# Where in an expert's pass the next expert's tokens are gathered and its registers loaded

## What is computed

```python
D_MODEL, SEQ, N_EXPERTS, TOP_K, D_FF_2 = 1024, 256, 32, 4, 1024
logits = t @ w_router + b_router
top_val, top_idx = lax.top_k(logits, TOP_K)
gate_w = jax.nn.softmax(top_val, axis=-1)
# for every expert e, over the tokens that chose it:
hb = xb @ w_exp_in[e] + b_exp_in[e]             # 1024 -> 2048
g = jnp.minimum(hb[:, :D_FF_2], 7.0)
u = jnp.clip(hb[:, D_FF_2:], -7.0, 7.0)
a = g * jax.nn.sigmoid(1.702 * g) * (u + 1.0)
y_e = a @ w_exp_out[e] + b_exp_out[e]           # 1024 -> 1024
# y[token] = sum over its 4 experts of gate_w * y_e
```

## Time and profile before

| | |
|---|---|
| time, median of 3 runs | 1464.12 us (1462.02 to 1468.61) |
| time of the profiled execution | 1462.36 us |
| span of the profiled execution | 1460.5 us |
| granted TensorE clock, mean over the span | 0.974 |
| PE busy | 1306.9 us, 89% of the span |
| DVE, ACT, POOL busy | 466.8, 504.1, 221.5 us |
| transfers | 494.40 MB, mean 339 GB/s |

### The profile page before, as it was taken

How to read it: one execution, slowest core, us unless ns; L and a number is a source line. 1 busy time by engine, 2 the same in 40 slices (tenths; PEclk the granted TensorE clock), 3 DMA queues, 4 the chain that set the end, 5 groups by cost and what they waited for, 6 DMA issues and landing times.

```text
span 1460.5 us, 25988 instructions
## 1 busy us (share of the span) xinstructions
PE 1306.9 (89%) x9475; PEld 810.3 (55%) x9476; DVE 466.8 (32%) x916; ACT 504.1 (35%) x790; POOL 221.5 (15%) x129
## 2 busy tenths in 40 slices
PE   7999999999999997787889898989888988898886
PEld 7787999878999853333333433344343434343433
DVE  2755777664534961111101110111011111111112
ACT  5566666555657422112111311131121212131222
POOL 6772122007774300000000000000000000000000
PEclk9999999999999999999999989999999999999999
DMA  9432667755463778999999999999999999999996
GB/s 342 171 101 64 185 186 234 281 194 182 165 231 116 270 331 373 431 432 430 431 431 404 431 431 431 415 432 431 431 431 431 420 431 431 431 418 431 431 431 268
DMA packets 105321, 494.40 MB, mean 339 GB/s; under 512 B 6609, under 2 KB 56129, under 8 KB 80481
## 3 DMA queue, kind: packets, MB, share of 16 engines
q1 hardware_dynamic: 103795, 491.50, 82.8%
q10 hardware_dynamic: 1486, 2.34, 0.4%
HBM read 492.76 MB, written 1.06 MB: 338 GB/s over the span
## 4 chain that ended last, share of the span: by engine, by line
PE 61%; DMA 25%; DVE 5%; ACT 4%; issue 3%; POOL 1%; SPq 0%; DVEq 0%; ACTq 0%; POOLq 0%
DMA big_mem<-in_w_exp_in 25%; PE ps L1071 18%; PE ps L1115 8%; PE ps L595 6%; PE ps L597 5%; PE ps L596 5%; PE ps L1054 3%; PE ps L1129 1%; PE ps L813 1%; PE ps L814 1%; PE ps L815 1%; PE ps L1138 1%; PE ps L1102 1%; ACT x L1740 1%; PE ps L615 1%
## 5 line engine op out<-in xcount | busy, mean ns | idle before, releaser
L1071 PE MATMUL ps<-big_mem,ring_mem 128*32 128x512 f32 (+1 forms) x2304 | 375.7, 623 | 46.5 <-DMA big_mem<-in_w_exp_in 46.4
L1071 PEld LDWEIGHTS ps<-big_mem,ring_mem 128*32 128x32 f32 (+1 forms) x2304 | 115.1, 124 | 288.6 <-issue 212.5
L1115 PE MATMUL ps<-big_mem,x 128*32 128x256 f32 (+1 forms) x1888 | 183.4, 436 | 4.7 <-ACT x L1740 3.7
L595 PE MATMUL ps<-hT_hi,w_hi 128*128 128x256 f32 x600 | 171.3, 285 | 1.3 <-DVE hT_lo L1836 1.3
L1724 ACT ACTIVATE ring_mem<-ring_mem 128x256 f32<-128x256 f32 (+1 forms) x36 | 17.7, 493 | 441.6 <-DVE ring_mem L2344 441.6
L596 PE MATMUL ps<-hT_lo,w_hi 128*128 128x256 f32 x600 | 169.7, 283 | 0.0
L597 PE MATMUL ps<-hT_hi,w_lo 128*128 128x256 f32 x600 | 169.7, 283 | 0.0
L1054 PEld LDWEIGHTS ps<-ring_mem,h 128*128 128x128 f32 x1024 | 124.0, 191 | 57.8 <-issue 57.8
L2344 DVE TENSOR_SCALAR ring_mem<-ps 128x256 f32<-128x256 f32 (+1 forms) x36 | 18.7, 520 | 406.6 <-PE ps L1071 406.6
L1795 ACT ACTIVATE big_mem<-ahead 128x2048 f32<-128x2048 f32 x62 | 115.0, 1902 | 85.2 <-DMA ahead<-in_w_exp_in 82.6
L1054 PE MATMUL ps<-ring_mem,h 128*128 128x96 f32 x1024 | 141.6, 281 | 0.0
(11 more groups left out here) (431 smaller groups left out, 1748.9 us busy)
## 6 DMA issues: line engine op xcount, KB each, us to landing
big_mem<-in_w_exp_in SPq DMA_DIRECT2D x97, 2048.0 KB, 23.1
big_mem<-in_w_exp_out SPq DMA_DIRECT2D x64, 2048.0 KB, 19.0
ahead<-in_w_exp_in SPq DMA_DIRECT2D x31, 2048.0 KB, 21.7
ring_mem<-in_w_in SPq DMA_DIRECT2D x14, 2048.0 KB, 7.7
ring_mem<-in_w_up SPq DMA_DIRECT2D x44, 512.0 KB, 4.9
ring_mem<-in_w_down SPq DMA_DIRECT2D x5, 2048.0 KB, 10.7
ring_mem<-in_w_out SPq DMA_DIRECT2D x4, 2048.0 KB, 7.7
ring_mem<-in_w_branch_a SPq DMA_DIRECT2D x1, 2048.0 KB, 7.3
```

The costliest lines, as they stand in the source:

```text
L595: mm(out, hi, x_hi, start=start, stop=False)
L1071: last = mm(out, stationary, weights[:, f, w * q:w * (q + 1)] if m > XS else weights[:, :, w * q:w * (q + 1)], start=start, stop=stop)
L1115: last = mm(ps[m * q:m * (q + 1), 4 + at // XS, 0:w], aT[:, k % n, k // n, :], wout[:, k, w * q:w * (q + 1)], start=(k == 0), stop=(k == K ...
```

## The change

Of `gather(0, EARLY)`, blocks 0 to 2 stay where they were; block 3 goes between `way_back` and `turn_a`, block 4 behind `turn_a`. Block 5 moves from ahead of `second` to behind it, blocks 6 and 7 both behind `combine`. `load_next` goes from behind the first gather to the very end of the pass. ACT copies blocks 0 to 4 after `a_in` rather than after the first sigmoid. No work is added or taken away.

```diff
@@ PE, one_pass
                 pe.wait_ge(s["picks_ready"], turn + 2)
-                gather(0, EARLY)
-                load_next()
+                gather(0, 3)
                 for b, (at, m) in enumerate(blocks):
                     pe.wait_ge(s["source_ready"], base + b + 1)
                     pe.wait_ge(s["u_ready"], base + b + 1)
                     way_back(b, at)
+                gather(3, EARLY - 1)
                 for b, (at, m) in enumerate(blocks):
                     pe.wait_ge(s["back_ready"], base + b + 1)
                     pe.wait_ge(s["a_ready"], base + b + 1)
                     turn_a(at, m)
+                gather(EARLY - 1, EARLY)
+                pe.wait_ge(s["aT_ready"], base + len(blocks))
+                second(blocks, landed_all)
                 pe.wait_ge(s["xT_ready"], 2 * turn + 3)
                 gather(EARLY, EARLY + 1)
-                pe.wait_ge(s["aT_ready"], base + len(blocks))
-                second(blocks, landed_all)
-                gather(EARLY + 1, EARLY + 2)
                 for b, (at, m) in enumerate(blocks):
                     pe.wait_ge(s["y_ready"], base + b + 1)
                     combine(b, at, m, base + b)
-                gather(EARLY + 2, KD)
+                gather(EARLY + 1, KD)
+                load_next()
                 pe.reg_add(base_reg, base_reg, len(blocks))
@@ ACT, one_pass
                 sigmoid(base, *blocks[0])
-                tokens_in(0, EARLY, 2 * turn + 3)
                 for b, (at, m) in enumerate(blocks):
...
                 for b, (at, m) in enumerate(blocks):
                     a_in(base + b, at, m)
+                tokens_in(0, EARLY, 2 * turn + 3)
```

## The result

| | before | after |
|---|---|---|
| time, median of 7 runs each, measured together | 1466.08 us | 1469.06 us (1468.34 to 1474.04) |
| ratio, after to before | | 1.0037, 95% interval 1.0021 to 1.0053 |
| profiled execution: time, span | 1462.36, 1460.5 us | 1471.93, 1470.1 us |
| granted TensorE clock, mean over the span | 0.974 | 0.949 |

The change makes the kernel slower by 0.37%, between 0.2 and 0.5%, some 3 to 8 us; I had forecast 1475 in a range of 1457 to 1489.

The account below looks back on a forecast made before the run. Weights bound the expert stage (907 us), PE having some 85 us to spare; after the change PE's 859 + 64 for the clock, 938 with stops and bias, give 1473.3 profiled, 1475 us predicted, range 1457 to 1489.

Parts of the forecast that it names:

- The gain between the matmuls: Between a pass's two matmuls, fewer gather rows and no load issue: -1.7, -1.15, -0.75 us for 32, 64, 96 slots.
- The loss at the end: At the pass's end, uncovered register loads delay the next pass: +2.7, +2.1, +3.0 us for 32, 64, 96 slots.
- Rival 2: At pass boundaries the loads stay covered: boundary grows at most 0.7 us, holes close, 1458 us; chance 0.08.
- PE becomes the bound: Expert stage: PE's 859 us plus 64 for the clock give 923 us, against 907 for the weights.
- nearly level: Expert stage: PE and weights nearly level, each sometimes waiting for the other; +11 us on the profiled execution.
- Rival 3: PE falls clearly behind the weights, every pass losing 3.0 us to the clock at its start: 1505 us; chance 0.06.
- rival 1: Expert stage: weights stay the bound if the clock mostly holds, holes shrink: -3.6 us, 1459 us; chance 0.31.
- GB/s below 429 in many slices: Sign that the forecast is right: transfer rate under 429 in many slices, no longer only around 96-slot passes.
- The clock: At most boundaries the clock falls, slowing the next pass's first matmul: 2.0 us a pass, 64 us in all.
- The sum: Expert stage 859 + 64 = 923 us, 938 with stops and bias; profiled time 1473.3 us, median 1475.
- stops and bias: Outside the passes: two sequencer waits at first-entered code, about 10 us, and bias matmuls, 3.4 and about 2 more.
- the last pass to have no boundary behind it: End of the stage: no gap of 3.4 + 2.7 us follows the last pass, so 6.1 us come off.

Follow-up runs that it names:

- e13: Changed kernel with `load_next` moved from the end of the pass to between gather block 5 and `combine`: 1460.6 us, ratio 0.9978 to before.
- e5: Changed kernel plus four dense float32 matmuls ahead of the loads at the end of 32-slot and 96-slot passes: 1460.7 us, ratio 0.9971 to before.
- e12: Changed kernel plus four dense matmuls ahead of the loads in the 32-slot passes alone: 1460.5 us, ratio 0.998 to before.
- e1: Changed kernel with the register loads alone back between the shortened first gather and the transposes: 1459.49 us, ratio 0.9957 to before.
- e3: Changed kernel with the three register loads split over the first matmul, ahead of k-slices 4, 5 and 6: 1461.05 us, ratio 0.9975 to before.
- e2: Kernel before with only `load_next` moved to the end of the pass: 1496.54 us, ratio 1.0214 to before.
- e6: Changed kernel with a second `load_next()` behind the first: 1558.92 us, ratio 1.0652 to before.

## Why the prediction was right, and what was mis-sized

**The gain between the matmuls was right.** Predicted -1.7, -1.15 and -0.75 us for 32, 64 and 96 slots. From the end of the first matmul to the start of `second` it went from 4.93 to 3.11, from 5.37 to 4.31 and from 5.99 to 5.04 us: -1.8, -1.1 and -0.95.

**The loss at the end was right.** Predicted +2.7, +2.1 and +3.0, an idle boundary of 2.9 us. From the end of `second` to the next pass it is 2.7, 2.1 and 3.1 us longer, and the idle time ahead of a 32-slot pass, behind one of 32 or 96 slots, is 2.84 to 2.96 but for the one-off stop. Rival 2 (loads covered) asked for less than 1.5 and is out; e13 shows that it needs no more than another place.

**That PE becomes the bound was right** (the wait for `w_exp_in` fell from 46.5 us to 1.4), and so was "nearly level": the last pass still waits 0.65 us for `w_exp_in` and 1.06 for `w_exp_out`. Rival 3 is out, and rival 1 needs the clock to hold: e5 and e12 are rival 1 made true by force, at ratios of 0.9971 and 0.998, where its -3.6 us make 0.9975.

One sign that I had named did not come: GB/s below 429 in many slices, no longer only around 96-slot passes. The rate stays at 430 between them, and the delay of all the passes shows only there, where the holes were before.

**The clock was the right mechanism with too large a size.** I took 2.0 us in each of 32 passes, 64 in all. The first matmul at full clock takes 7.3, 14.4 and 22.9 us for 32, 64 and 96 slots. Taking these from the lengths of all 32 in after leaves 53 us, of which 1.4 are waits for weights: the clock took 52. A single fall cost more than I had said, 2.4 us on the mean, but there were 22 of them and not 32; the other passes began at full clock. Behind a 64-slot pass, whose `combine` is one piece and whose boundary has 1.62 us idle, the clock did not fall save at the one-off stop; I had put the term in at every pass.

**The sum.** The stage, to the end of the last `second`, was predicted to take 859 + 64 + 15 - 6.1 = 931.9 us and took 927.8. By terms: the passes at full clock 863 instead of 859 (a 32-slot pass takes 20.5 on the mean, not 20.3, a 64-slot pass 31.4, not 31.25), the clock 52 instead of 64, stops and bias 15 as forecast, and 4 us of waits for weights that I had not put in; less the 6.1 that makes 928, the measured stage. So the one large error, 12 us of clock, was in part made up by two small ones of the other sign. That the span came out within 1.3 us of the forecast is partly luck: the stage is 4.1 us shorter than I had it, what lies ahead of it and is not touched by the change was 1.3 us longer in this execution, and what lies behind it is 1.5 longer.

Those 1.5 us are a term that I had put at nothing: I took the last pass to have no boundary behind it. But its loads still hold up PE's sequencer, which then comes to the end of the program (L130) as the last of the engines, 1.5 us behind SP; in before it was there 1.2 us ahead of SP. From the end of the last `second` to the end of the span it is 12.0 us in before, e1 and e3, 13.5 in after and e2, and 15.9 in e6. The rows at L130, of before and then of after:

```profile
L130 PEldq DRAIN  x1: 8/8/8, 1459.1 to 1459.1; - x1
L130 SPq DRAIN  x1: 7/7/7, 1460.3 to 1460.3; - x1
...
L130 SPq DRAIN  x1: 7/7/7, 1468.4 to 1468.4; - x1
L130 PEldq DRAIN  x1: 8/8/8, 1469.9 to 1469.9; - x1
```

The median came out 6 us below the 1475: 1.4 of them in the profiled time (1471.93, forecast 1473.3), the rest because the profiled execution lies 2.9 us above its median, where I had added 1.8. As a change, I had forecast 11 us, 0.75%; the ratio says 0.37%, half of it. Three slips of arithmetic in the prediction carry nothing: 31 times 29.3 is 908 and not 907, 545.92 - 544.73 is 1.19 and not 1.15, and rival 3 comes to 1507 by its own terms, not 1505.

**What the clock and a load cost.** The slow starts took 52 us of a span of 1470, 3.5%. In the time they show as the step from 1.0037 to 0.9971 between after and e5, some 10 us, because the weights take over as soon as PE is that much faster. The Trainium skill (TensorE: Matmul & The Clock Gate, Part 1) puts the ramp's penalty at under 1% of a typical kernel's span; it says so where it speaks of the ramp at a kernel's start, and the prediction tried it on a ramp at every boundary. For that the trace does not agree: it is 3.5% in PE's time, though no more than 0.7% in the kernel's. One load lasts 0.30 us after the change too, and the three with their register work 2.4 to 2.7; the floor of about 600 ns that the Trainium skill gives (DMA: Bandwidth & Descriptors, Latency and other measured facts) is again not what the trace shows.

## What to carry to other kernels

Register loads cost the part of their time that no matmuls queued ahead of them cover: put them where many matmuls are queued and no wait on the engine's own result stands just in front, not between the last matmul of a loop body and its branch. Before moving an engine that has time to spare, work out how much each pass may grow before it becomes the bound (here 2.7 us), and count what a gap costs the clock as well as the gap. A small dense filler can be cheaper than the gap that it fills.

## What the runs showed that I had not expected

- Four added matmuls (3.6 us of PE time in each of 23 passes) made the changed kernel 0.7% faster (a ratio of 0.9971 to before, against 1.0037) by keeping the granted clock at 0.991 instead of 0.949.
- The sequencer covers 2.7 us of register work with surprisingly little: in e1 the first MOVE executes at 947.2, 1.6 us before `gu` ends, and the rest lies under 12 gather rows of 0.12 us, so that `way_back` has no idle time; the last third of `second` covers two thirds of it in e13.
- After a gap of the same length the first matmul took 7.04 us in one pass and 9.44 in another, with 2.87 and 2.88 us of idle time: whether the clock falls is not decided by the length of the gap alone. What else decides it stays open.
